# Cross-attention: the low parts of heads 1 to 3 made by VectorE in place of GpSimd

## The reference, cut to what matters

```python
def cross_attention(xn, mk, mv, w_xq, xq_norm, w_xo):
    bsz, t, _ = xn.shape
    q = rmsnorm((xn @ w_xq).reshape(bsz, t, N_HEADS_X, HEAD_DIM_X), xq_norm)
    s = jnp.einsum('bqhd,bkhd->bhqk', q, mk).astype(jnp.float32) * (HEAD_DIM_X ** -0.5)
    p = jax.nn.softmax(s, axis=-1).astype(mv.dtype)
    o = jnp.einsum('bhqk,bkhd->bqhd', p, mv).reshape(bsz, t, N_HEADS_X * HEAD_DIM_X)
    return o @ w_xo
```

## Time and profile before

| | us |
|---|---|
| median of 3 runs | 1684.39 |
| the profiled execution's own time | 1680.23 |
| its span | 1678.5 |
| mean granted TensorE clock over the span | 0.973 |
| TensorE busy | 1585.2 |
| VectorE busy | 1012.9 |
| GpSimd busy | 305.2 |

### The profile page before, as it was taken

One profiled execution on the slowest core, in us unless ns is written; L12 is line 12 of the kernel. 1 busy time (PEld: TensorE's weight loads), 2 busy tenths in 40 slices (PEclk: granted clock), 3 DMA queues, 4 the chain that ended last, 5 costly groups with the idle time before them and its releaser, 6 DMA issues.

```text
span 1678.5 us, 27557 instructions
## 1 busy us (share of the span) xinstructions
PE 1585.2 (94%) x11172; PEld 1545.9 (92%) x11172; DVE 1012.9 (60%) x1481; ACT 653.5 (39%) x1146; POOL 305.2 (18%) x354
## 2 busy tenths in 40 slices
PE   6999999997888899999779999999999999999999
PEld 6999999995777799998669999999999999999999
DVE  6625876536888754225653477666666658656653
ACT  5521021126787632214552253333333433333332
POOL 1011000002221010000430004444444421010110
PEclk8999999987999999999999999999999999999999
DMA  7424111002110043201042214433334586454563
GB/s 241 143 89 159 50 39 38 26 1 92 36 37 33 26 138 138 89 26 51 1 148 100 90 55 152 147 143 141 142 142 166 202 281 235 123 165 147 155 211 114
DMA packets 63667, 189.36 MB, mean 113 GB/s; under 512 B 7873, under 2 KB 13049, under 8 KB 63409
## 3 DMA queue, kind: packets, MB, share of 16 engines
q1 hardware_dynamic: 37904, 91.11, 17.1%
q0 software_dynamic: 25648, 96.65, 16.0%
HBM read 138.58 MB, written 54.12 MB: 115 GB/s over the span
## 4 chain that ended last, share of the span: by engine, by line
PE 81%; DVE 7%; ACT 5%; DMA 4%; issue 3%; POOL 1%; SPq 0%; ACTq 0%; DVEq 0%; POOLq 0%
PE ps L452 33%; PE ps L2605 19%; PE ps L2626 17%; PE ps L2163 3%; PE ps L481 2%; DMA a<-wdn 2%; PE ps L2504 2%; PE ps L2356 1%; ACT scores L1168 1%; PE ps L2334 1%; DVE pt_lo L1759 1%; PE ps L2472 1%; PE ps L503 1%; PE ps L2318 1%; DVE scores L1738 1%
## 5 line engine op out<-in xcount | busy, mean ns | idle before, releaser
L452 PE MATMUL ps<-A_hi,w_hi 128*128 128x364 f32 x768 | 174.0, 335 | 0.0
L452 PE MATMUL ps<-A_lo,w_hi 128*128 128x364 f32 x768 | 171.1, 331 | 0.0
L452 PE MATMUL ps<-A_hi,w_lo 128*128 128x364 f32 x768 | 170.7, 331 | 0.0
L393 DVE TENSOR_TENSOR w_lo<-w_raw,w_hi 128x1024 fp32r<-128x1024 f32 x43 | 52.5, 1223 | 150.0 <-ACT w_hi L389 149.6
L389 ACT ACTIVATE w_hi<-w_raw 128x1024 fp32r<-128x1024 f32 x42 | 44.3, 1057 | 241.7 <-PE ps L452 136.2
L452 PEld LDWEIGHTS ps<-A_lo,w_hi 128*128 128x128 f32 x768 | 135.1, 190 | 0.0
L452 PEld LDWEIGHTS ps<-A_hi,w_lo 128*128 128x128 f32 x768 | 135.0, 190 | 0.0
L452 PEld LDWEIGHTS ps<-A_hi,w_hi 128*128 128x128 f32 x768 | 134.2, 191 | 0.0
L2605 PE MATMUL ps<-t_hi,wq_hi 128*128 128x272 f32 x480 | 99.9, 290 | 2.3 <-DVE hid_stage L2059 2.3
L2605 PE MATMUL ps<-t_lo,wq_hi 128*128 128x272 f32 x480 | 99.9, 290 | 0.0
L2605 PE MATMUL ps<-t_hi,wq_lo 128*128 128x272 f32 x480 | 99.7, 289 | 0.0
(11 more groups left out here) (342 smaller groups left out, 4087.6 us busy)
## 6 DMA issues: line engine op xcount, KB each, us to landing
w_raw<-slabs SPq DMA_DIRECT2D x68, 512.0 KB, 4.0
quads_d<-quad_sum POOLq DMA_DIRECT2D x64, 272.0 KB, 2.9
w_raw<-wdn POOLq DMA_DIRECT2D x32, 512.0 KB, 4.0
r_raw_a<-quads_d SPq DMA_DIRECT2D x56, 272.0 KB, 3.1
r_raw_b<-quads_d SPq DMA_DIRECT2D x56, 272.0 KB, 3.0
quads_d<-hid_stage POOLq DMA_DIRECT2D x48, 272.0 KB, 2.9
Y<-xT POOLq DMA_DIRECT2D x16, 546.0 KB, 4.6
y_d<-Y POOLq DMA_DIRECT2D x16, 546.0 KB, 3.2
```

What stands on the lines that cost most here:

```text
L393: e.tensor_tensor(WL[:, par], RAW[:, par], WH[:, par].bitcast(F32), ALU.subtract).then_inc(s.w_lo, 1)
L452: ins = e.matmul(PS[:, 3 * par + c, 0:CH], wt[:, wpar, w], xt[:, col:col + CH], start=(first and n == 0 and m == 0), stop=(last and n == l ...
```

## The change

The twelve calls of `x_lo_part` on GpSimd are removed. VectorE makes the same twelve low parts, each one iteration after ScalarE made the high part, at the end of its iteration `u`: behind `xpt_lo` and `xo_lo` of that iteration, and in iteration 3 ahead of the reciprocal and the norm of head 3. So VectorE makes parts 0 and 1 of head 1 in iteration 1, part 2 in iteration 2 and part 3 in iteration 3; head 2's four parts in iterations 4 to 7; head 3's parts 0 and 1 in iteration 11, part 2 in 12 and part 3 in 13. Semaphores, buffers and all other orders stay.

```diff
--- before.py
+++ after.py
@@ -890,9 +890,6 @@
 
             g.wait_ge(s.xkv_lo, 2)
             g.wait_ge(s.xq_lo, 2)
-            for u in sorted(X_SPLIT):
-                for h, part in X_SPLIT[u]:
-                    x_lo_part(g, h, part)
             g.wait_ge(s.xq_lo, 8)
             g.wait_ge(s.y1_out, 128)
             for k in range(KT):
@@ -1959,6 +1956,8 @@
                 if done is not None:
                     xo_lo(done)
                 done = q if last else None
+                for h, part in X_SPLIT.get(u - 1, ()):
+                    x_lo_part(e, h, part)
                 if u == 3:
                     dve_recip(e, cnt)
                     xq_nrm(3, (0, 1, 2))
```

## The result

The changed kernel took 1696.49 us, the median of 4 runs (1691.94 to 1697.02), against 1682.85 us for the kernel before (4 runs, 1681.21 to 1684.91). The ratio is 1.0077, with a 95% interval from 1.0041 to 1.0114: slower by 13.0 us (0.77% of 1682.85), with 6.9 to 19.2 inside the interval. A second series gave 1.0082 (1.0058 to 1.0107). The forecast was 1694.0 in 1687 to 1700. It stood on 1684.4 for the kernel before, which took 1682.85 in this comparison: so the time was missed by 2.5 us, but the difference, +9.6 against +13.0, by 3.4.

A forecast was written before the change was run, and what follows sets the result against it. The prediction took the heads stage to be bound by a ring of engines waiting in turn, not by a full engine. It summed 3.9 + 3.3 + 2.4 = +9.6 us onto 1684.4, giving 1694.0, range 1687 to 1700.

The forecast's parts named there:

- What bounds: Heads stage: engines wait in a ring, none full; new work stands behind VectorE's waits for ScalarE, so idle time is past.
- Prices of the work: VectorE's two kinds of low part: 1.29 and 1.19 us from head 0, taken as 1.2 each, 14.4 in all.
- Head 1: Iterations 1 to 3: query parts cost nothing, part 2 makes unit 5's scores 2.7 us late, part 3 adds 1.2; +3.9.
- the hold: Normalising product at 797.37, under two GpSimd query parts, takes 2.44 us against a 0.69 median; 1.75 of 3.3 us of holding.
- Head 2: Iterations 4 to 7: 2.4 from the first two, less 0.3 of slack, iteration 6 covered, 1.2 from iteration 7; +3.3 us.
- Head 3: Iterations 11 to 13: maximum 0.9 us late, then part 2 delays unit 15's scores 2.4, part 3 free; +2.4.
- The sum of the steps: Heads stage: 3.9 + 3.3 + 2.4 = +9.6 us for the three heads.
- Queues: GpSimd's eight row reloads behind the parts start about 853.7 and cost nothing; SyncE's loads move with the ring.
- The clock: TensorE in the heads stage: slow 1.2 GHz stretches cost 1.6 us each; none charged, +3.2 or -1.6 possible.
- VectorE fills its idle time: Rival, heads stage: parts fall into VectorE's waits, relief of holds and TensorE's wait makes it faster, 1679.7 us; chance 0.05.
- Nearly nothing: Rival, heads stage: ScalarE's and TensorE's slack takes up all but 3 us, 1687 or less; chance 0.09.
- All of it and the clock: Rival, heads stage: no cover holds anywhere, 14.4 + 3.2 = 17.6 us, 1702; chance 0.06.

The follow-up runs named there:

- the GpSimd kernel with cut parts: Kernel before with the twelve GpSimd parts cut to 16 columns and low parts of heads 1 to 3 left out of the products; ratio 1.0006 (0.9977 to 1.0036).
- the second pair: Kernel before and changed kernel, both unchanged, each profiled once more; heads stages 96.6 and 110.8 us.
- three covered parts: Kernel before with only head 1's part 0 and head 3's parts 0 and 3 on VectorE, nine left on GpSimd; ratio 0.9999 (0.9979 to 1.0019).
- the two mended ones: Kernel before with only head 3's first query part and prompt keys and values on VectorE, iterations 11 and 12; ratio 0.9996 (0.9971 to 1.0022).

## Why the prediction was right, point by point

**What bounds.** Right. The stage is a ring, the added work stood behind VectorE's waits, and the waits stayed (26.3 of 27.1 us).

**Prices of the work.** Right: 1.29 and 1.22 us. The second was 0.03 over head 0's.

**Head 1** (+3.9). The links gave 3.80. Parts 0 and 1 cost nothing, as said. The cover was as I had counted it: with the hold the product ended 1.70 ahead of its transposes (799.81, 801.51), the hold gave 1.75 more, and the two parts took 2.40. The hold by itself was worth nothing: the GpSimd kernel with cut parts shows that `xo_lo(0)` comes no earlier without it.

**Head 2** (+3.3). The links gave 3.21, with 1.20, 1.20, -0.30 and, for iterations 6 and 7, 1.11.

**Head 3** (+2.4). The links gave 2.32, 0.84 of it at the maximum of unit 14 (0.9 forecast). The part of iteration 13 was covered.

**The sum of the steps.** 9.3 us against 9.6. That is the part of the forecast that was right for its reason, step by step.

**Queues.** Right in kind: the reloads cost nothing. They started at 855.11, 857.6 with the 2.45 added, where I had 853.7. The 3.9 between are the slow products up to there (3.6), which I had left out, and 0.3. The last one started at 885.13, well ahead of the first residual at 914.00.

**The clock** is the term that was mis-sized. I took none, "since the gaps mostly move", and put 3.2 into the range; it measured 3.9, and 4.9 in the second pair. The difference was missed by 3.4, and the clock accounts for it: the parts made 0.3 less than forecast. The gaps do not only move: the two ahead of units 5 and 15 are new or longer (2.75 and 3.27 us), and products behind them ran at 1.2 GHz: 2.90 us in place of 1.65 behind the first. A slow stretch can also cost more than the 1.6 that I read from the earlier trace rows: a value product wholly inside one took 5.50 us against 3.03.

**Rivals.** "VectorE fills its idle time" failed by its own test, since the added work ahead of released products was 1.1 to 1.2 and not under 0.3. The Trainium skill, GPSIMD Engine Reference, section "Key points", names contention of GpSimd with VectorE instructions that have two SBUF inputs. The trace agrees: the products at 797.37 and 844.08, which began well inside a GpSimd part, took 2.44 and 2.21 us, and 0.69 once GpSimd's parts were gone. My argument from the median of 0.69 was no evidence against it: sixteen of the twenty products do not begin inside a GpSimd part at all, and two more begin in its last 0.2 us. The relief was real on VectorE's row, but it was worth nothing on the ring. "Nearly nothing" failed too: the parts pushed the links by 9.3 us, and only 0.30 of slack, at `xpt_lo(3)`, came off them on the way. "All of it and the clock" (17.6) was the nearest of the three to the 13.2 and had the clock right in kind, but its reason was wrong: iterations 1, 6, 11 and 13 kept most of their cover.

## What to carry to other kernels

In a stage where the engines wait for one another in turn, price a moved instruction by the link behind it and by the wait in front of it on its new engine, not by the engine's idle share: one part of 1.2 us ahead of a released product made it 2.7 us late and cost 4.5 us of measured time (1.3 to 7.7), three covered parts none that could be measured (-3.5 to 3.2). Then add a term for the clock of TensorE wherever the move opens or lengthens one of its gaps; here it was 3.9 to 4.9 on top of 9.3. And a contention that shows on an engine's row is worth its removal only if the next link starts earlier without it.

## What the runs showed of the hardware

The two held products of the kernel before ended 0.55 and 0.54 us behind GpSimd's parts (799.81 and 846.29, against 799.26 and 845.75), and alone each takes 0.69: so they did nearly all of their work only after GpSimd had ended. A hold also hits moved parts: where nine parts stayed on GpSimd, a query part on VectorE took 1.74 and 1.66 us in place of 1.29. Further, filling a gap took away the slow stretch right behind it and no more: the mean clock of the stage went from 0.86 to 0.87, at 5 us more of TensorE's busy time. Which small shift moves a slow stretch onto a value product stays open. It can be as large as what one sets out to measure: with three covered parts slow products took 3.6 us in the one profiled execution, and with the two mended ones they took 1.3 us back.
